# Attention values as the stationary operand of the probability products, two heads at a time, with transposed output, in a hybrid decoder layer; and a reordered entry of attention

## The chip, the cores and the metric

The kernel runs on one core of one Trainium2 chip. The metric is device time in microseconds. Five engines of the core have queues of their own and meet only at semaphores: TensorE (PE in the profile; PEld is its loading of the stationary operand), VectorE (DVE), ScalarE (ACT), GpSimd (POOL) and SyncE (SP), which here only issues transfers.

## The reference

One layer of a hybrid decoder on x (512 positions, 1024 features), all float32: RMS norm; one projection to all inputs of two mixers; (A) a gated linear recurrence, 4 heads of 128; (B) sparse attention, 8 heads of 64: an indexer scores all keys, each query keeps its best 128, and their logits get a bias by distance; the outputs of both mixers concatenated times W_o, normalised and added to x; then a SwiGLU feed-forward of 2816 hidden features, normalised and added. What the change is about:

```
p = softmax(logits)                    # per query, over the kept keys
y_B[q, h, :] = sum_k p[q, h, k] * v[k, h, :]
y = concat(y_A, y_B) @ w_o
```

## The kernel before

**Projections.** The 512 positions are 4 blocks of 128. Weights arrive in chunks of 1 MB (`chunks`, index j) through a ring of two raw buffers. Each is split in two float32r parts: ScalarE copies the rounded value to `w_hi`, VectorE subtracts to get `w_lo` (`split(j)`); a product with such operands takes three passes (`passes`). 33 `groups` of 128 features (24 passes of 512 columns each, some 5.5 us) are projected by `project(g)`; ScalarE and VectorE evacuate group g (`evac`, for keys and queries also `stack_lo`) out of PSUM bank g % 4. The last four groups, 29 to 32, are the attention keys, two heads each.

**Top-k.** VectorE finds the best 128 keys by 16 rounds for each of three query blocks (`topk_round`: maximum of eight, replace). `topk_share(g)` says how many of the 48 rounds VectorE does at each group from 7 on: three to group 12, then two. Groups 14 to 20 carry also the seven levels of the recurrence, for which VectorE (`advance`) and ScalarE (`level_operands`) prepare operands of TensorE (L1215).

**Attention** is a software pipeline over 32 units (b, h), `unit_order`, written out by hand in the same order on all engines. Step i (`attend(i)`) does, on TensorE: the logits of unit i (L1191, L1192); the probability product of unit i - 5 (L1333); the turning of unit i - 3's probabilities through the identity (L1344). GpSimd makes a tile of bias and mask for each unit (L523), three buffers. VectorE adds it and finds the row maximum (L993), ScalarE takes the exponential and its sum (L664), and the two alternate in copying turned probabilities to SBUF (L320, L667). In block b a unit has b + 1 tiles of 128 keys.

The product of a unit has the turned probabilities as stationary operand (128 keys x 128 queries) and the 64 value columns moving; the block's result is y with queries on partitions. When all eight heads of a block are done (`block_done`), VectorE multiplies by the reciprocal sums (`y_norm_b`, L978 a reciprocal of 8 elements a partition, L982), TensorE turns the result by four transposes (`turn_y_b`, L1304), ScalarE and VectorE make its two parts for the output projection (`y_hi_b`, `y_lo_b`). The recurrence's parts (`y_hi_a`, `y_lo_a`) and the split of the first W_o chunk in quarters (`split_quarter`, L550 and L795) are placed at fixed steps.

Steps 0 to 5 of TensorE lie between the passes of the last group; ScalarE and VectorE do steps 0 to 4, then that group's evacuation, then go on.

**Down projection.** Eleven chunks; the last chunk is done for row blocks 0 to 3 in turn, block 3 in two halves of 512 columns. Each block is then squared on ScalarE, its inverse root taken on GpSimd (L442), multiplied (L1125, or L1131 for halves), scaled and added (L1135) on VectorE, and stored.

Of the kernel before, what the change touches and what calls it, by code (L numbers as in the profile page):

```python
# [34 lines left out]
def hymba_layer(nc, x, w_in, lb_logits, hgrn_gnorm, rel_bias, w_o, norm_pre_mix, norm_post_mix,  # L35
# [54 lines left out]
    EARLY = HEADS_B - 2  # L90
    unit_order = [(b, h) for b in range(TB) for h in range(HEADS_B)]
    unit_order[EARLY:EARLY + 5] = [(1, 0), (1, 1), (1, 2), (0, EARLY), (0, EARLY + 1)]
    Y_A_AT = {12 + 2 * h: h for h in range(HEADS_A)}
    QUARTER_AT = {22: 0, 24: 1, 26: 2, 28: 3}
    TURN_BANK = (4, 6, 4, 2)

    with ExitStack() as ctx:
# [13 lines left out]
        N1, N2 = FT * 2 * S, 7936  # L111
# [29 lines left out]
        rs = sb("rs", [P, UNITS])  # L141
# [22 lines left out]
        PT = [a1(21504 + 512 * i, 512) for i in range(2)]  # L164
        yb = [a1(2048, 512), a1(2560, 512)]
# [16 lines left out]
        raw_ikw = A2[:, 7296:7296 + KT * IKW]  # L182
        Bh = A2[:, 0:4096].rearrange("p (h c) -> p h c", h=HEADS_B)
# [74 lines left out]
        s_yb = sem("attention_y_normed")  # L258
        s_ybt = sem("attention_yT_psum")
# [4 lines left out]
        s_woq = sem("quarter_of_first_wo_hi")  # L264
# [22 lines left out]
        def qk_bank(i):  # L287
            return 6 if i % 3 == 2 and i < unit_order.index((0, EARLY)) else QK_BANK[i % 3]

# [77 lines left out]
        def slot_free(eng, j):  # L367
            before = [i for i in range(j) if w_slot(i) == w_slot(j)]
            if before:
                used(eng, before[-1])  # L370
            elif w_slot(j) == 2:
                eng.wait_ge(s_pv, UNITS)
# [166 lines left out]
        def _(act):  # L539
# [5 lines left out]
            def split_quarter(q):  # L545
                if q == 0:
                    raw_landed(act, J_WO)
                    slot_free(act, J_WO)
                cols = slice(q * CH // 4, (q + 1) * CH // 4)
                act.activation(w_hi[:, w_slot(J_WO), cols], raw[:, ring_of(J_WO) % 2, cols],  # L550
                               ACT.Copy).then_inc(s_hi if q == 3 else s_woq, 1)

# [44 lines left out]
            def evac(g):  # L597
# [13 lines left out]
                elif kind == "ak":  # L611
                    for e in range(2):
# [93 lines left out]
            for i in range(EARLY - 1, UNITS + PV_LAG):  # L706
                attend(i)
            y_hi_b(TB - 1)
# [67 lines left out]
        def _(dve):  # L776
# [12 lines left out]
            def split_quarter(q):  # L789
                if q == 3:  # L790
                    dve.wait_ge(s_hi, J_WO + 1)
                else:
                    dve.wait_ge(s_woq, q + 1)
                cols = slice(q * CH // 4, (q + 1) * CH // 4)
                o = dve.tensor_tensor(w_lo[:, w_slot(J_WO), cols], raw[:, ring_of(J_WO) % 2, cols],  # L795
                                      w_hi[:, w_slot(J_WO), cols].bitcast(F32), ALU.subtract)
                if q == 3:
                    o.then_inc(s_lo, 1)

# [116 lines left out]
            def stack_lo(g):  # L916
# [5 lines left out]
                for e in range(1 if kind == "ikw" else 2):  # L922
# [10 lines left out]
                o.then_inc(s_ev[g % 4], 1)  # L933
# [35 lines left out]
            def y_lo_b(b):  # L969
                dve.wait_ge(s_yhi, b + 1)  # L970
                dve.tensor_tensor(hT_lo[:, 4:8, b * P:(b + 1) * P],
                                  PS[:, 6, :].rearrange("p (k t) -> p k t", t=P),
                                  hT_hi[:, 4:8, b * P:(b + 1) * P].bitcast(F32), ALU.subtract).then_inc(s_ylo, 1)

            def y_norm_b(b):
                u = slice(8 * b, 8 * b + 8)
                dve.wait_ge(s_ex, ended(b))
                link(dve.reciprocal(rs[:, u], sm[:, u]))  # L978
                dve.wait_ge(s_pv, ended(b))
                if b >= 2:  # L980
                    dve.wait_ge(s_ybt, b - 1)
                dve.tensor_tensor(yb[b % 2].rearrange("p (h d) -> p h d", d=DH),  # L982
                                  PS[:, 4 + b % 2, :].rearrange("p (h d) -> p h d", d=DH),
                                  rs[:, u].unsqueeze(2).to_broadcast([P, HEADS_B, DH]), ALU.mult).then_inc(s_yb, 1)

            def attend(i):
# [12 lines left out]
                if i - 1 in QUARTER_AT:  # L999
                    split_quarter(QUARTER_AT[i - 1])  # L1000
                b = block_done(i - 1)
                if b is not None:
                    y_norm_b(b)
# [485 lines left out]
```

## Time and profile before

| | us |
|---|---|
| median of 3 timed runs (703.04, 706.20, 706.27) | 706.2 |
| profiled execution, own time | 704.14 |
| its span, first to last instruction | 702.4 |
| TensorE busy / VectorE / ScalarE / GpSimd | 685.9 / 381.9 / 259.8 / 93.9 |
| mean granted TensorE clock | 0.997 |

Busy times of engines overlap each other. On TensorE a record's end is modelled and lies over the start of the next record, so the distance of two starts is what a pass takes. An fp32 product is recorded as two matmuls, a transpose as one. "Idle before" is the time in which an engine had nothing running ahead of the instruction.

### The profile page before, as it was taken

The numbers are of one execution on the slowest core, as the hardware profiler recorded it, in microseconds if no ns is written. First come the engines' busy times: TensorE is split into PE (matmuls) and PEld (weight loads), VectorE is DVE, ScalarE is ACT, GpSimd is POOL, SyncE is SP. The second block draws the span as 40 slices with busy tenths as digits, with TensorE's granted clock in tenths as the row PEclk, the third lists the DMA queues.
The fourth block names the chain that finished last, engine by engine and source line by source line (L and its number), as shares of the span: only waits on it lengthen the run. The fifth ranks groups of instructions, "written<-read, shape, count | busy, mean of one in ns | idle before, by whom it ended". The sixth has DMA issues, their size and how long they took to land.

```text
span 702.4 us, 8568 instructions
## 1 busy us (share of the span) xinstructions
PE 685.9 (98%) x3472; PEld 579.0 (82%) x3472; DVE 381.9 (54%) x553; ACT 259.8 (37%) x401; POOL 93.9 (13%) x130
## 2 busy tenths in 40 slices
PE   8999999999999979999999999999999999999996
PEld 5978888888988878888988888888888888888884
DVE  3865999999668689337643343343433432212216
ACT  5656434444257377235532223133232231211213
POOL 1810220000407478002100000000000000000001
PEclk9999999999999999999999999999999999999998
DMA  8443042342521100351350332323313223233103
GB/s 261 122 150 87 35 120 61 105 159 67 181 61 60 61 1 30 152 185 55 97 170 9 115 114 68 119 75 105 120 61 119 96 85 119 64 116 112 69 0 120
DMA packets 49352, 68.59 MB, mean 98 GB/s; under 512 B 5025, under 2 KB 39841, under 8 KB 49314
## 3 DMA queue, kind: packets, MB, share of 16 engines
q1 hardware_dynamic: 44320, 60.07, 26.6%
q0 software_dynamic: 3280, 7.35, 3.0%
q10 hardware_dynamic: 1714, 0.64, 0.4%
q8 instruction: 27, 0.44, 0.2%
q14 instruction: 11, 0.09, 0.0%
HBM read 65.40 MB, written 4.74 MB: 100 GB/s over the span
## 4 chain that ended last, share of the span: by engine, by line
PE 81%; DVE 12%; ACT 4%; issue 3%; DMA 0%; POOL 0%; DVEq 0%; ACTq 0%
PE PS L1143 70%; PE PS L1333 2%; DVE w_lo L787 2%; DVE A L858 2%; DVE top L857 1%; DVE A L1031 1%; PE PS L1252 1%; PE PS L1215 1%; PE PS L1186 1%; PE PS L1344 1%; PE PS L1239 1%; PE PS L1192 1%; ACT A L702 1%; PE PS L1191 1%; PE PS L1276 1%
## 5 line engine op out<-in xcount | busy, mean ns | idle before, releaser
L1143 PE MATMUL PS<-hT_lo,w_hi 128*128 128x512 f32 (+2 forms) x584 | 218.3, 374 | 0.9 <-DVE w_lo L819 0.5
L1143 PE MATMUL PS<-hT_hi,w_lo 128*128 128x512 f32 (+2 forms) x584 | 217.2, 372 | 0.0
L1143 PE MATMUL PS<-hT_hi,w_hi 128*128 128x512 f32 (+2 forms) x584 | 217.2, 372 | 0.0
L787 DVE TENSOR_TENSOR w_lo<-raw,w_hi 128x2048 fp32r<-128x2048 f32 x49 | 114.5, 2336 | 176.0 <-ACT w_hi L543 175.7
L543 ACT ACTIVATE w_hi<-raw 128x2048 fp32r<-128x2048 f32 x49 | 93.8, 1914 | 210.2 <-PE PS L1143 209.5
L1143 PEld LDWEIGHTS PS<-hT_lo,w_hi 128*128 128x128 f32 (+1 forms) x584 | 109.7, 188 | 20.1 <-DVE w_lo L819 0.8
L1143 PEld LDWEIGHTS PS<-hT_hi,w_hi 128*128 128x128 f32 (+1 forms) x584 | 109.6, 188 | 19.5
L1143 PEld LDWEIGHTS PS<-hT_hi,w_lo 128*128 128x128 f32 (+1 forms) x584 | 109.7, 188 | 18.5
L1143 PE MATMUL PS<-w_hi,ff 128*128 128x512 f32 x352 | 108.2, 389 | 0.0
L1143 PEld LDWEIGHTS PS<-w_hi,ff 128*128 128x128 f32 x352 | 66.1, 188 | 13.7
L1143 PE MATMUL PS<-w_lo,ff 128*128 128x512 f32 x176 | 68.5, 389 | 0.0
L442 POOL TENSOR_TENSOR rstd<-ms,mhalf 128x1 f32<-128x1 f32 x16 | 10.3, 642 | 423.7 <-ACT ms L722 406.9
L1143 PE MATMUL PS<-w_lo,hT_hi 128*128 128x512 f32 x112 | 44.6, 398 | 0.0
L1143 PE MATMUL PS<-w_hi,hT_hi 128*128 128x512 f32 x112 | 43.7, 390 | 0.0
L1143 PE MATMUL PS<-w_hi,hT_lo 128*128 128x512 f32 x112 | 43.6, 390 | 0.0
L1104 DVE TENSOR_TENSOR A<-PS,A 128x512 f32<-128x512 f32 x22 | 15.2, 692 | 47.2 <-issue 27.6
L1143 PEld LDWEIGHTS PS<-w_lo,ff 128*128 128x128 f32 x176 | 33.0, 188 | 6.9
L931 DVE SCALAR_TENSOR_TENSOR QK<-PS,QK 64x512 fp32r<-64x512 f32 x33 | 22.7, 689 | 11.6 <-ACT QK L609 6.7
L857 DVE MAX8 top<-A 128x8 f32<-128x256 f32 (+2 forms) x48 | 26.7, 557 | 0.6
L523 POOL TENSOR_TENSOR A<-A 128x256 f32<-128x256 f32 (+2 forms) x24 | 26.0, 1105 | 7.2 <-DVE nm L993 6.9
L858 DVE MATCH_REPLACE8 A<-top,A 128x256 f32<-128x256 f32 (+2 forms) x48 | 26.0, 543 | 0.0
L1333 PEld LDWEIGHTS PS<-A 128*128 128x128 f32 x160 | 21.3, 191 | 4.9 <-ACT A L667 4.1
(170 smaller groups left out, 762.3 us busy)
## 6 DMA issues: line engine op xcount, KB each, us to landing
raw<-in_w_in_dram SPq DMA_DIRECT2D x16, 1024.0 KB, 5.6
raw<-in_w_gate_dram SPq DMA_DIRECT2D x11, 1024.0 KB, 5.2
raw<-in_w_up_dram SPq DMA_DIRECT2D x11, 1024.0 KB, 5.3
raw<-in_w_down_dram SPq DMA_DIRECT2D x11, 1024.0 KB, 4.9
raw<-in_w_o_dram SPq DMA_DIRECT2D x4, 1024.0 KB, 4.9
A<-in_x_dram SPq DMA_DIRECT2D x4, 512.0 KB, 5.6
A<-in_x_dram POOLq DMA_DIRECT2D x4, 512.0 KB, 7.4
out_dram<-A SPq DMA_DIRECT2D x8, 256.0 KB, 2.0
```

The lines of the kernel that those rows point to most:

```text
L442: pool.tensor_tensor(rstd[:, col:col + 1], ms[:, col:col + 1], mhalf[:, 0:1], ALU.pow).then_inc(s_rs, 1)
L523: pool.tensor_tensor(BM[u % 3][:, 0:n], M, Bh[:, h, (TB - 1 - b) * P:S], ALU.subtract).then_inc(s_bm, 1)
L543: act.activation(w_split(j)[0], raw_view(j), ACT.Copy).then_inc(s_hi, 1)
L702: o = act.activation(junk[:, i % 8 * DK:(i % 8 + 1) * DK], ya[:, i * DK:(i + 1) * DK], ACT.Square, accum_out=ss[:, 16 + i:17 + i])
L787: dve.tensor_tensor(lo, raw_view(j), hi.bitcast(F32), ALU.subtract).then_inc(s_lo, 1)
L857: link(dve.max(top8[:, :], SC[b]))
L858: link(dve.match_replace(SC[b], top8[:, :], SC[b], TAKEN))
L931: o = dve.scalar_tensor_tensor(out=t, in0=p, scalar=scale, in1=hi, op0=ALU.mult, op1=ALU.subtract)
L1031: o = dve.scalar_tensor_tensor(out=SC[b], in0=rl[u % 3][:, 0:n], scalar=iw[:, b, h:h + 1], in1=SC[b], op0=ALU.mult, op1=ALU.add)
L1104: dve.tensor_tensor(fraw[f % 2], PS[:, 2 + f % 2, :], sig[f % 2], ALU.mult).then_inc(s_fr, 1)
L1143: o = pe.matmul(out, lhs[a], rhs[b], start=(first and n == 0), stop=(last and n == 2))
L1333: o = pe.matmul(PS[:, 4 + b % 2, h * DH:(h + 1) * DH], PT[u % 2][:, s * P:(s + 1) * P], av[:, s * W + h * DH:s * W + (h + 1) * DH], start= ...
```

## The change

The product of a pair of units (h, h + 1) of one block is now issued together, at every second step: the values of one head (128 keys x 64) are stationary, the turned probabilities (128 queries) move. Head h writes PSUM partitions 0 to 63, head h + 1 partitions 64 to 127 (two halves of the array), so that the block's result comes out transposed. The turned probabilities get four buffers instead of two.

The transposes of y go. The reciprocal sums must now lie along the columns: VectorE writes them widened to 64 copies a head (`widen_sums`, a reciprocal with 128 x 512 outputs), TensorE turns them by four fp32 products with the identity (`spread_sums`), ScalarE copies them to SBUF (`take_sums`), and VectorE multiplies (`y_norm_b`).

The order of units is (0, 0..5), (1, 0..5), (0, 6..7), (1, 6..7), then blocks 2 and 3. Steps 0 to 3 lie between the passes of group 31, steps 4 to 8 between those of group 32 (`BESIDE`), with the evacuation of each in two halves around a step. The first W_o chunk is split whole, after group 30, and the recurrence's parts are made from step 23. `topk_share` gives one round a group from 13 to 20, and three from 22 to 25.

In the down projection the last two chunks are done together for each row block; all 24 passes of each half of block 3 come last.

```diff
-    EARLY = HEADS_B - 2
-    unit_order = [(b, h) for b in range(TB) for h in range(HEADS_B)]
-    unit_order[EARLY:EARLY + 5] = [(1, 0), (1, 1), (1, 2), (0, EARLY), (0, EARLY + 1)]
-    Y_A_AT = {12 + 2 * h: h for h in range(HEADS_A)}
-    QUARTER_AT = {22: 0, 24: 1, 26: 2, 28: 3}
+    unit_order = [(b, h) for b in (0, 1) for h in range(HEADS_B - 2)]
+    unit_order += [(b, h) for b in (0, 1) for h in (HEADS_B - 2, HEADS_B - 1)] + [(b, h) for b in range(2, TB) for h in range(HEADS_B)]
+    LAST_KEYS = unit_order.index((0, HEADS_B - 2))
+    BESIDE = {len(groups) - 2: (4, range(4)), len(groups) - 1: (3, range(4, 9))}
+    Y_A_AT = {23 + 2 * h: h for h in range(HEADS_A)}
...
-        PT = [a1(21504 + 512 * i, 512) for i in range(2)]
-        yb = [a1(2048, 512), a1(2560, 512)]
+        PT = [a1(21504, 512), a1(22016, 512), a1(2560, 512), a1(3584, 512)]
+        y_sb = [a1(2048, 512), A2[:, 7936:8448]]
...
         def turned_to_sbuf(eng, u, copy):
             n = (unit_order[u][0] + 1) * P
             eng.wait_ge(s_ptp, u + 1)
-            if u >= 2:
-                eng.wait_ge(s_pv, u - 1)
-            copy(PT[u % 2][:, 0:n], PS[:, 2 + u % 2, 0:n]).then_inc(s_pts[u % 2], 1)
+            if u >= 4:
+                eng.wait_ge(s_pv, (u - 4) // 2 + 1)
+            copy(PT[u % 4][:, 0:n], PS[:, 2 + u % 2, 0:n]).then_inc(s_pts[u % 2], 1)
...
-            def evac(g):
+            def evac(g, heads=(0, 1)):
...
+            def take_sums(b):
+                act.wait_ge(s_rps, b + 1)
+                if b >= 2:
+                    act.wait_ge(s_ylo, b - 1)
+                act.activation(y_sb[b % 2], PS[:, 6, :], ACT.Copy).then_inc(s_rsb, 1)
+
             def y_hi_b(b):
-                act.wait_ge(s_ybt, b + 1)
+                act.wait_ge(s_yb, b + 1)
                 act.activation(hT_hi[:, 4:8, b * P:(b + 1) * P],
-                               PS[:, 6, :].rearrange("p (k t) -> p k t", t=P), ACT.Copy).then_inc(s_yhi, 1)
+                               y_sb[b % 2].rearrange("p (k t) -> p k t", t=P), ACT.Copy).then_inc(s_yhi, 1)
 
...
-                if i in QUARTER_AT:
-                    split_quarter(QUARTER_AT[i])
-                b = block_done(i - 3)
+                b = block_done(i - 2)
+                if b is not None:
+                    take_sums(b)
+                b = block_done(i - 4)
                 if b is not None:
                     y_hi_b(b)
...
-                if g + 1 == len(groups):
-                    for i in range(EARLY - 1):
+                if g in BESIDE:
+                    units = BESIDE[g][1]
+                    for i in units[:-1]:
                         attend(i)
-                evac(g)
-                if last_of_chunk(g) and j + 2 < J_WO and j + 2 != AHEAD:
+                    evac(g, (0,))
+                    attend(units[-1])
+                    evac(g, (1,))
+                else:
+                    evac(g)
+                if last_of_chunk(g) and j + 2 <= J_WO and j + 2 != AHEAD:
                     split(j + 2)
...
             def topk_share(g):
-                if g < G_L0 - 1:
+                if g < G_L0 - 1 or G_OFF <= g <= G_YNORM:
                     return (1, 2) if last_of_chunk(g) else (2, 1)
-                return (1, 1)
...
             def y_lo_b(b):
                 dve.wait_ge(s_yhi, b + 1)
-                dve.tensor_tensor(hT_lo[:, 4:8, b * P:(b + 1) * P],
-                                  PS[:, 6, :].rearrange("p (k t) -> p k t", t=P),
+                dve.tensor_tensor(hT_lo[:, 4:8, b * P:(b + 1) * P], y_sb[b % 2].rearrange("p (k t) -> p k t", t=P),
                                   hT_hi[:, 4:8, b * P:(b + 1) * P].bitcast(F32), ALU.subtract).then_inc(s_ylo, 1)
 
+            def widen_sums(b):
+                dve.wait_ge(s_ex, ended(b))
+                if b:
+                    dve.wait_ge(s_rps, b)
+                dve.reciprocal(r_wide.rearrange("p (h d) -> p h d", d=DH),
+                               sm[:, 8 * b:8 * b + 8].unsqueeze(2).to_broadcast([P, HEADS_B, DH])).then_inc(s_rw, 1)
+
             def y_norm_b(b):
-                u = slice(8 * b, 8 * b + 8)
-                dve.wait_ge(s_ex, ended(b))
-                link(dve.reciprocal(rs[:, u], sm[:, u]))
-                dve.wait_ge(s_pv, ended(b))
-                if b >= 2:
-                    dve.wait_ge(s_ybt, b - 1)
-                dve.tensor_tensor(yb[b % 2].rearrange("p (h d) -> p h d", d=DH),
-                                  PS[:, 4 + b % 2, :].rearrange("p (h d) -> p h d", d=DH),
-                                  rs[:, u].unsqueeze(2).to_broadcast([P, HEADS_B, DH]), ALU.mult).then_inc(s_yb, 1)
+                dve.wait_ge(s_rsb, b + 1)
+                dve.wait_ge(s_pv, ended(b) // 2)
+                dve.tensor_tensor(y_sb[b % 2], PS[:, 4 + b % 2, :], y_sb[b % 2], ALU.mult).then_inc(s_yb, 1)
...
                 feature_group(w_split(0), m, P, m, S // 2, S, s_proj)
-            def turn_y_b(b):
-                pe.wait_ge(s_yb, b + 1)
-                if b >= 1:
-                    pe.wait_ge(s_ylo, b)
+            def spread_sums(b):
+                pe.wait_ge(s_rw, b + 1)
+                if b:
+                    pe.wait_ge(s_rsb, b)
                 for k in range(4):
-                    o = pe.transpose(PS[:, 6, k * P:(k + 1) * P], yb[b % 2][:, k * P:(k + 1) * P], ident[:, :])
-                o.then_inc(s_ybt, 1)
+                    o = pe.matmul(PS[:, 6, k * P:(k + 1) * P], r_wide[:, k * P:(k + 1) * P], ident[:, :],
+                                  start=True, stop=True)
+                o.then_inc(s_rps, 1)
...
+                if i >= PV_LAG and (i - PV_LAG) % 2:
                     u = i - PV_LAG
-                    b, h = unit_order[u]
-                    pe.wait_ge(s_pts[u % 2], u // 2 + 1)
-                    if u == 0:
+                    b, h = unit_order[u - 1]
+                    for e in range(2):
+                        pe.wait_ge(s_pts[e], u // 2 + 1)
+                    if u == 1:
                         for g in range(first_group["av"], first_group["av"] + 4):
                             evacuated(pe, g)
                     if h == 0 and b >= 2:
                         pe.wait_ge(s_yb, b - 1)
                     for s in range(b + 1):
-                        o = pe.matmul(PS[:, 4 + b % 2, h * DH:(h + 1) * DH], PT[u % 2][:, s * P:(s + 1) * P],
-                                      av[:, s * W + h * DH:s * W + (h + 1) * DH], start=(s == 0), stop=(s == b))
+                        for e in range(2):
+                            o = pe.matmul(PS[e * DH:(e + 1) * DH, 4 + b % 2, h // 2 * P:(h // 2 + 1) * P],
+                                          av[:, s * W + (h + e) * DH:s * W + (h + e + 1) * DH],
+                                          PT[(u - 1 + e) % 4][:, s * P:(s + 1) * P], start=(s == 0), stop=(s == b))
                     o.then_inc(s_pv, 1)
...
                     elif c == 0 and t == 1:
                         pe.wait_ge(s_pts[0], UNITS // 2)
                         pe.wait_ge(s_pts[1], UNITS // 2)
+                        spread_sums(TB - 1)
                     elif c == 0 and t == 2:
-                        turn_y_b(TB - 1)
+                        pe.wait_ge(s_yb, TB)
                     elif c == 0 and t == 3:
                         pe.wait_ge(s_ylo, TB)
...
+            C_LAST = FT // 2 - 1
+            for c in range(C_LAST - 1):
                 pe.wait_ge(s_lo, J_DN + c + 1)
                 pe.wait_ge(s_flo, 2 * c + 2)
...
+            pe.wait_ge(s_flo, FT)
+            pe.wait_ge(s_lo, J_DN + C_LAST)
+            for t in range(2):
+                row_block(J_DN + C_LAST - 1, 2 * C_LAST - 2, ff_parts, t, False, False)
+            pe.wait_ge(s_lo, J_DN + C_LAST + 1)
+            for t in range(2):
+                row_block(J_DN + C_LAST, 2 * C_LAST, ff_parts, t, False, True).then_inc(s_dn, 1)
+            row_block(J_DN + C_LAST - 1, 2 * C_LAST - 2, ff_parts, 2, False, False)
+            row_block(J_DN + C_LAST, 2 * C_LAST, ff_parts, 2, False, True).then_inc(s_dn, 1)
+            t = TB - 1
+            for half in range(2):
+                for k in range(2 * C_LAST - 2, 2 * C_LAST + 2):
+                    w = w_split(J_DN + k // 2)
+                    o = passes(k, [x[:, t * P:(t + 1) * P] for x in ff_parts(k)],
+                               [x[:, k % 2, half * 512:(half + 1) * 512] for x in w],
+                               PS[:, 2 * t + half, :], False, k == 2 * C_LAST + 1)
+                o.then_inc(s_dn, 1)
```

## Rows read from the trace of the kernel before

**Rows 1.** The page: busy time and share; shares of the chain that ended last.
```profile
PE 685.9 (98%) x3472; PEld 579.0 (82%) x3472; DVE 381.9 (54%) x553; ACT 259.8 (37%) x401; POOL 93.9 (13%) x130
...
PE 81%; DVE 12%; ACT 4%; issue 3%; DMA 0%; POOL 0%; DVEq 0%; ACTq 0%
```

**Rows 2.** Windows: stretch, busy us of PE, PEld, DVE, ACT, POOL; granted clock; DMA share.
```profile
160.00:175.00 15.00, 15.00 (x85) 12.99 (x84) 14.72 (x33) 5.44 (x7) 0.00 (x0) 1.00 0.24 71
190.00:205.00 15.00, 15.00 (x81) 12.88 (x80) 7.74 (x12) 3.60 (x5) 0.00 (x0) 1.00 0.05 13
240.00:288.00 48.00, 43.34 (x338) 39.96 (x337) 35.72 (x103) 33.37 (x94) 30.48 (x33) 1.00 0.17 67
```

**Rows 3.** What TensorE waited for over the whole span: us, times, longest.
```profile
PE PS L1333 <- ACT A L667: 3.0, 3, 2.0
...
PE PS L1304 <- DVE A L982: 1.7, 2, 1.1
PE PS L1215 <- ACT A L645: 1.5, 2, 0.8
```

**Rows 4.** TensorE in order of time in attention: start, length, [idle before <-releaser].
```profile
246.53 0.28 PE L1192 MATMUL PS<-QK 128*128 128x256 f32 x1
248.81 0.43 PE L1333 MATMUL PS<-A 128*128 128x64 f32 x2 [2.00 <-ACT A L667]
...
258.76 0.66 PE L1304 MATMUL PS<-ident,A 128*128 128x128 f32 x4 [1.09 <-DVE A L982]
...
263.65 0.55 PE L1333 MATMUL PS<-A 128*128 128x64 f32 x3 [0.77 <-ACT A L667]
...
279.37 0.66 PE L1304 MATMUL PS<-ident,A 128*128 128x128 f32 x4 [0.59 <-DVE A L982]
279.78 0.47 PE L1191 MATMUL PS<-QK 128*128 128x512 f32 x1
```

**Rows 5.** TensorE in order of time, two units of block 3.
```profile
281.15 0.61 PE L1344 MATMUL PS<-ident,A 128*128 128x128 f32 x4
281.59 1.00 PE L1333 MATMUL PS<-A 128*128 128x64 f32 x8
282.43 0.60 PE L1344 MATMUL PS<-ident,A 128*128 128x128 f32 x4
```

**Rows 6.** Line 1252, fp32 products of 128 columns: count, lengths, first and last start.
```profile
L1252 PE MATMUL PS<-A x80: 270/275/275, 183.7 to 192.6; 128*128 128x128 f32 x80
```

**Rows 7.** TensorE in order of time around the eight-row transposes.
```profile
52.09 0.39 PE L1143 MATMUL PS<-hT_hi,w_hi 128*128 128x512 f32 x1
52.41 0.41 PE L1199 MATMUL PS<-ident,A 8*128 8x8 f32 x4
```

**Rows 8.** VectorE by line and shape: count, busy us, mean ns, idle before.
```profile
L993 DVE CUSTOM_DVE_ANT_0 A<-PS,A 128x384 f32<-128x384 f32 x8 | 4.3, 551 | 0.9 <-PE PS L1192 0.8
...
L795 DVE TENSOR_TENSOR w_lo<-raw,w_hi 128x512 fp32r<-128x512 f32 x4 | 3.9, 978 | 0.6 <-ACT w_hi L550 0.5
...
L982 DVE TENSOR_TENSOR A<-PS,rs 128x512 f32<-128x512 f32 x4 | 2.8, 692 | 1.2 <-issue 1.1
...
L978 DVE RECIPROCAL rs<-sm 128x8 f32<-128x8 f32 x4 | 0.8, 192 | 0.0
...
L842 DVE RECIPROCAL lbw<-lbw 128x4 f32<-128x4 f32 x1 | 0.2, 178 | 0.0
```

**Rows 9.** GpSimd by line and shape from 236 to 300 us.
```profile
L523 POOL TENSOR_TENSOR A<-A 128x512 f32<-128x512 f32 x8 | 11.0, 1404 | 1.7 <-DVE nm L993 1.6
```

**Rows 10.** The end of the kernel in order of time.
```profile
695.84 0.60 ACT L765 ACTIVATE raw<-PS 128x512 f32<-128x512 f32 x1 [0.44 <-PE PS L1143]
...
696.93 0.65 POOL L442 TENSOR_TENSOR rstd<-ms,mhalf 128x1 f32<-128x1 f32 x1 [1.84 <-ACT ms L771]
697.09 1.41 DVE L1131 TENSOR_TENSOR raw<-PS,A 128x512 f32<-128x512 f32 x2
698.54 1.42 DVE L1135 SCALAR_TENSOR_TENSOR A<-raw,rstd,A 128x512 f32<-128x512 f32 x2
```

More of the change, by code:

```diff
@@ L287, in qk_bank @@
         def qk_bank(i):
-            return 6 if i % 3 == 2 and i < unit_order.index((0, EARLY)) else QK_BANK[i % 3]
+            return 6 if i % 3 == 2 and i < LAST_KEYS else QK_BANK[i % 3]
         def ended(b):
@@ L611, in evac @@
                 elif kind == "ak":
-                    for e in range(2):
+                    for e in heads:
                         act.activation(KS[0:DH, 2 * h + e, :], ps[e * DH:(e + 1) * DH, :], ACT.Copy).then_inc(s_sth, 1)
@@ L704, in _ @@
                     o.then_inc(s_ss, 1)
-            for i in range(EARLY - 1, UNITS + PV_LAG):
+            for i in range(9, UNITS + PV_LAG):
                 attend(i)
+            take_sums(TB - 1)
             y_hi_b(TB - 1)
@@ L921, in stack_lo @@
                 scale = -DH ** -0.5 if kind == "aq" else 1.0
-                for e in range(1 if kind == "ikw" else 2):
+                for e in heads[:1] if kind == "ikw" else heads:
                     dve.wait_ge(s_sth, before + (2 if kind == "ikw" else e + 1))
@@ L1035, in _ @@
                     split(j + 2)
-                if g + 1 == len(groups):
+                if g in BESIDE:
                     topk_rounds(48)
-                    for i in range(EARLY - 1):
+                    units = BESIDE[g][1]
+                    for i in units[:-1]:
                         attend(i)
-                evac(g)
+                    stack_lo(g, (0,))
+                    attend(units[-1])
+                    stack_lo(g, (1,))
+                else:
+                    evac(g)
                 if g >= G_TOPK:
@@ L1059, in _ @@
                     topk_rounds(topk_share(g)[1])
-            for i in range(EARLY - 1, UNITS + PV_LAG):
+            for i in range(9, UNITS + PV_LAG):
                 attend(i)
+            widen_sums(TB - 1)
             y_norm_b(TB - 1)
@@ L1159, in beside @@
                     return lambda k: indexer_dot(g, k)
-                if g + 1 == len(groups):
-                    return lambda k: attend(k + EARLY - KT) if k >= KT - EARLY else None
+                if g in BESIDE:
+                    k0, units = BESIDE[g]
+                    return lambda k: attend(units[k - k0]) if 0 <= k - k0 < len(units) else None
                 return None
@@ L1362, in _ @@
                     turn_y()
-            for i in range(EARLY, UNITS + PV_LAG):
+            for i in range(9, UNITS + PV_LAG):
                 attend(i)
@@ L1430, in _, with ff_parts @@
                     feature_group(w_split(j), m, P, 2 * up + m, S // 2 if c == 0 else 0, S, s_gu)
[L1431 removed]
+            def ff_parts(k):
+                return ff[:, k, 0, :], ff[:, k, 1, :]
+            C_LAST = FT // 2 - 1
+            for c in range(C_LAST - 1):
                 pe.wait_ge(s_lo, J_DN + c + 1)
                 pe.wait_ge(s_flo, 2 * c + 2)
[L1434 removed]
                 for t in (2, 3, 0, 1) if c == 0 else range(TB):
@@ L1438, in _ @@
                         pe.wait_ge(s_fr, FT)
-                    def acts(k):
-                        return ff[:, k, 0, :], ff[:, k, 1, :]
-                    if last and t == TB - 1:
-                        w = w_split(J_DN + c)
-                        for half in range(2):
-                            for kk in range(2):
-                                o = passes(kk, [x[:, t * P:(t + 1) * P] for x in acts(2 * c + kk)],
-                                           [x[:, kk, half * 512:(half + 1) * 512] for x in w],
-                                           PS[:, 2 * t + half, :], False, kk == 1)
-                            o.then_inc(s_dn, 1)
-                        continue
-                    o = row_block(J_DN + c, 2 * c, acts, t, c == 0, last)
-                    if last:
-                        o.then_inc(s_dn, 1)
-                if not last:
-                    o.then_inc(s_rows, 1)
+                    o = row_block(J_DN + c, 2 * c, ff_parts, t, c == 0, False)
+                o.then_inc(s_rows, 1)
+            pe.wait_ge(s_flo, FT)
[15 more added lines that the diff above has]
+                o.then_inc(s_dn, 1)
     return nc
```

52 lines of the change are left out of this document (18 added, 34 removed).

## The prediction

> **What bounds the kernel now.** Read the page first: TensorE is busy for 98% of the span, and the chain that ended last runs through it for 81% [rows 1]. So only two things can shorten this kernel: less work in TensorE's own queue, or fewer places where that queue stands. "Busy" hides both, because the end of a matmul is modelled; from here on durations on TensorE are distances between starts. Next the stretches: in attention (240 to 288 us) TensorE is busy 43.3 of 48 us, VectorE 35.7, ScalarE 33.4, GpSimd 30.5, at the full granted clock [rows 2]; nobody is far behind, so a cut on TensorE soon meets somebody else. Then the waits of TensorE: 3.0 us on ScalarE's copies of turned probabilities (L667), 1.7 us on VectorE's normalisation (L982), 1.5 us on the operands of the recurrence's levels (L645) [rows 3]. The timeline places those of attention: 2.00 us at unit 7, 1.09 at block 0's turn, 0.77 in block 2, 0.59 at block 2's turn [rows 4]. Each is really 0.16 us longer (the record before it, 0.28 us long, fills a slot of 0.12), which with a last small one makes 5.4 us of standing. The first comes because ScalarE does the last group's evacuation between the softmax of units 4 and 5 while TensorE has nothing but attention left.
>
> **1. The probability products.** 80 fp32 products are 160 passes (a product is recorded as two matmuls). Today the probabilities are stationary with 128 columns and 64 columns stream: eight passes take 281.59 to 282.43 = 0.84 us, 0.105 each, 16.7 us in all [rows 5]. In the new form 64 columns are stationary and 128 stream. A pass with 128 fp32 columns costs (192.6 - 183.7)/79 = 0.112 us [rows 6]; so passes one after another cost 17.9 us, a small loss. The gain is there only if the two halves run at once. The order issued is head 0 pass a, pass b, head 1 pass a, pass b: within a head b follows a, but head 1's a may lie beside head 0's b. A pair of units of block b has 4(b+1) passes and then takes 2(b+1)+1 slots: 3, 5, 7, 9 for blocks 0 to 3, four pairs each, 96 slots x 0.112 = 10.8 us. No row shows two halves at once, so the bounds are 10.8 and 17.9; I take 10.8, since nothing else here can be what the form is limited by once passes address different columns.
>
> **2. Changing the shape of the array in use.** Each of 16 pairs has a change in and one out. The nearest row: from a 512-column pass at 52.09 to eight-row transposes at 52.41 is 0.32 us where the pass itself fills 0.23, so 0.09 for a change [rows 7]. 32 x 0.09 = 2.9 us (bounds 0 and, at 0.2 each, 6.4). Part 1 and 2 together: 13.7 against 16.7, -3.0 us.
> The Trainium skill speaks against this part: TensorEngine Tiling (Array Packing), Key Properties, says that changing the tiling mode drains the engine, while tiles of one mode work independently. By the trace the nearest such change costs 0.09 us, a modest drain; the page gives no figure, and no run so far shows a change of column tiles.
>
> **3. Spreading the reciprocal sums.** Sixteen transposes (four take 279.37 to 279.78 [rows 4], 1.65 us in all) go; 16 fp32 products, 32 passes x 0.112 = 3.6 us, come: +1.9 us. TensorE's own work changes by -1.1 us.
>
> **4. The widened reciprocal on VectorE.** Now a reciprocal of 8 elements takes 192 ns, one of 4 takes 178 [rows 8]. The new one has 512. At one element a cycle it would be 0.69 us, like the multiply of that size [rows 8]; if the whole 192 ns were per-element cost it would be 12 us. The two reciprocals differ by 3.5 ns an element: 0.18 + 508 x 0.0035 = 2.0 us, which I take. Four of them, W each.
> VectorE: DVE Perf Modes, in the Trainium skill (its walkthrough of the 8-slice pipeline), says that a reciprocal is an iterative divide with a repeat count of 8. At the 0.96 GHz that the skill's Trainium Kernel Development and Optimization (NeuronCore Architecture) gives for VectorE that would be, as an estimate, 8.3 ns an element and 4.3 us. The rows, at 3.5 ns an element, agree only in direction; rival (b) is the one that this rule speaks for, and with 4.3 its sum would be some 2.4 us higher.
>
> **5. The waits in attention afterwards.** Block 0's sums are widened at step 19 and TensorE wants them at step 20. From the logits of unit 19, VectorE needs 0.55 (one reduction [rows 8]) + W + 0.1. TensorE's pieces: turning is 0.11 a tile [rows 5], so 0.3 for three; logits are two passes of 384 columns at 0.23 for 512 [rows 7], so 0.4; a pair of block 1 is 5 x 0.112 + 0.18 = 0.7. It turns, forms logits, multiplies and turns, 1.7, and stands W - 1.0. At step 22 the first product of block 2 needs block 0's normalised result out of the same bank, and VectorE has on the way two reductions, a copy as wide, block 1's widening and the multiply (0.69, L982 [rows 8]), and it first waits 0.3 for the second logits: 2.7 + W, against TensorE's 0.9 of spreading, 0.4, 0.3 and 0.4: it stands W + 0.7. For block 2, with four tiles, TensorE's cover is 2.5 us against 0.8 + W: W - 1.7. Block 3's widening lies beside 2.7 us of output projection and a pair of products: nothing below W = 3. With W = 2.0: 1.0 + 2.7 + 0.3 = 4.0 us.
> Entry: nine units instead of six are beside the last two groups, and evacuation is cut in two around a unit, so the 2.16 us stand shrinks. Behind the whole split of the first output-weight chunk after group 30, unit 0's softmax comes some 0.3 us late, and the two evacuation halves hold units 9 to 12 by some 0.5: 0.8 us. The 0.77 us at 263.65 is ScalarE's two copies of earlier y parts; these move later and apart: 0. Altogether 4.8 instead of 5.4: -0.6 us. Four added copies on ScalarE replace four quarter splits, 512 wide like them. VectorE loses 4 x 0.98 of quarter splits (L795 [rows 8]) in attention and gains 4 W: 4.1 us more, paid in the waits just counted. GpSimd needs 1.40 us for a bias tile of block 3 [rows 9] beside a unit of TensorE of about 1.5: it hides, barely.
>
> **6. Top-k rounds moved.** Eight rounds leave the level stage, where VectorE is busy 14.7 of 15 us, and go to where it is busy 7.7 of 15 [rows 2]. The waits on L645 are for operands that VectorE releases: a round less in every group removes both, -1.5 us [rows 3]. Were they due to ScalarE, nothing.
>
> **7. The tail.** After the last matmul (its square starts at 695.84) the inverse root is ready at 696.93 + 0.65 = 697.58, but VectorE reaches the last scaling at 698.54, because it was busy with block 2's and then with two multiplies from 697.09 [rows 10]. With 24 matmuls instead of 12 behind block 2, block 2 and the first half are done by then: scaling starts near 697.65, -0.9 us. The next-to-last weights are needed 5.4 us earlier relative to the last ones, whose split ends with about 1 us to spare.
>
> **Sum.** -1.1 - 0.6 - 1.5 - 0.9 = -4.1 us against the profiled execution's 704.1: 700.0. That execution lies 2.1 below the median shown; the four times known average 704.9, and I place the changed kernel from there: 700.8 us.
>
> **Rivals.**
> (a) A cheap widening, W = 0.7: step 22 stands 1.4, the others nothing, so the stands are 2.2, -3.2 against today, and the sum is -6.7: 698.2 us. For it: the reciprocal of 4 elements is hardly dearer than other tiny instructions; against: the slope.
> (b) VectorE becomes the bound: W = 3.7, twice the slope. Stands of 2.7, 4.4, 2.0 and 0.7 with the entry 0.8 make 10.6, +5.2 against today, and the sum is +1.7: 706.6 us.
> (c) The halves do not overlap (slower): the products cost 17.9 + 2.9 = 20.8, +4.1, the spreading +1.9. A longer pair covers more of the waits (4.2, so -1.2), the rest stands: +2.4, 707.3 us with W = 2.0, and some +8 with 3.7. It decides once the overlap saves less than 4 of its 7.1 us. For it: every pass in this trace starts only when its predecessor's columns are through. Against: here all passes use all columns.
> (d) The products cost what I say but the level waits and the entry's merely move: 702 to 703 us.
>
> **How the numbers follow.** Forecast 0.33, (a) 0.18, (b) 0.21, (c) 0.23, (d) 0.05. From no change a measurement can tell about 0.5%, 3.5 us. The forecast lies just beyond that: some 0.20 of its 0.33 is faster; with (a) and 0.06 from (b) to (d), 0.44. Slower: half of (c), a third of (b), 0.18. Same 0.38. The likeliest case alone spans 698.5 to 703; for 8 in 10, 697 to 708.5, between a cheap reciprocal and serial halves.
>
> **What would show it.** Starts of products of two heads less than 0.06 us apart on average for right, 0.11 for (c). The reciprocal's own row for W. The waits of TensorE on VectorE near block 0 and 1 for step 5; no wait on L645; the last scaling under 2 us after the last matmul. It would be wrong if a change of shape costs 0.2 us, or if one of the longer stands lowers the granted clock, which is 1.00 now even with a stand of 2.2 us.

## The result, and the profile after

The changed kernel takes 720.9 us (median of four runs, 719.9 to 724.5) where the kernel before takes 705.7: ratio 1.0243, 95% interval 1.0208 to 1.0278. By the ratio it is 17 us slower; the two medians alone, few runs each, lie 15.1 us apart, and against the 704.2 us that the kernel before takes in the experiments the distance is 16.7. The prediction said 4 us faster, and its range ended at 708.5. The profiled execution took 724.5 us, the slowest of the four.

The page after: its busy times, which answer to [rows 1], and the 40 slices of TensorE and of its granted clock:
```profile
PE 695.1 (96%) x3488; PEld 580.4 (80%) x3488; DVE 393.1 (54%) x550; ACT 262.2 (36%) x402; POOL 92.0 (13%) x130
...
PE   8999999999999777799999999999999999999996
...
PEclk9999999999999997999999999999999999999999
```
TensorE falls behind in slices 14 to 17, 235 to 307 us: attention. The waits of TensorE in 220 to 330 us (engine, tile and line, what it waited for: us, times, longest), which answer to [rows 3]:
```profile
PE PS L1308 <- DVE A L974: 5.0, 2, 3.2
PE PS L1195 <- DVE A L908: 4.1, 1, 4.1
PE PS L1340 <- DVE A L980: 3.6, 1, 3.6
PE PS L1352 <- ACT A L666: 2.6, 2, 2.2
PE PS L1340 <- DVE A L321: 2.2, 3, 0.9
PE PS L1195 <- DVE QK L926: 1.3, 1, 1.3
```
ScalarE was the first to be waited for; now it is VectorE. L974 is the widened reciprocal, L908 the gating multiplications of the recurrence's output, L980 block 0's normalisation. The waits on the level operands (L645 before) are gone, as forecast. VectorE by line and shape, from 226 to 320 us, has the price of the first:
```profile
L974 DVE RECIPROCAL A<-sm 128x512 f32<-128x512 f32 x4 | 13.4, 3345 | 0.0
L793 DVE TENSOR_TENSOR w_lo<-raw,w_hi 128x2048 fp32r<-128x2048 f32 x3 | 7.1, 2381 | 1.2 <-ACT w_hi L544 1.1
```
That is 3.35 us, 6.5 ns an element, where 2.0 us was taken. The second is shown in VectorE's order of time, with what the moved top-k rounds (L852 to L855) do to L908:
```profile
235.29 0.68 DVE L853 MATCH_REPLACE8 A<-top,A 128x512 f32<-128x512 f32 x1
236.00 0.43 DVE L855 TENSOR_SCALAR A<-A 128x512 f32<-128x512 f32 x1
236.46 2.73 DVE L908 SCALAR_TENSOR_TENSOR A<-PS,gn,A 128x512 f32<-128x512 f32 x4
```
The same multiplications in the kernel before:
```profile
231.83 2.73 DVE L913 SCALAR_TENSOR_TENSOR A<-PS,gn,A 128x512 f32<-128x512 f32 x4
```
They start 4.6 us later now. The search ends at 236.4 us, and only then does VectorE reach what the first logit waits for. TensorE in order of time (start, length, idle before and releaser), to be laid beside [rows 4]:
```profile
239.24 0.33 PE L1195 MATMUL PS<-QK 128*128 128x128 f32 x1 [4.11 <-DVE A L908]
...
248.35 0.30 PE L1195 MATMUL PS<-QK 128*128 128x128 f32 x1 [1.30 <-DVE QK L926]
...
255.67 0.44 PE L1340 MATMUL PS<-A 128*64 128x128 f32 x4 [0.89 <-DVE A L321]
...
258.95 0.41 PE L1352 MATMUL PS<-ident,A 128*128 128x128 f32 x2 [2.24 <-ACT A L666]
...
271.15 2.08 PE L1308 MATMUL PS<-ident,A 128*128 128x128 f32 x8 [1.89 <-DVE A L974]
...
278.43 1.55 PE L1340 MATMUL PS<-A 128*64 128x128 f32 x12 [3.57 <-DVE A L980]
...
298.17 1.99 PE L1308 MATMUL PS<-ident,A 128*128 128x128 f32 x8 [3.16 <-DVE A L974]
```
These seven stands are 17.2 us as recorded; the four of [rows 4] were 4.5. The last, the widening of block 2 with 3.16 us, is longer than the reciprocal alone explains; VectorE's rows ahead of it show why:
```profile
293.65 1.20 DVE L963 TENSOR_TENSOR hT_lo<-A,hT_hi 128x512 fp32r<-128x512 f32 x1
294.77 3.34 DVE L974 RECIPROCAL A<-sm 128x512 f32<-128x512 f32 x1
```
L963 makes the low part of one head of the recurrence, which the change moved to steps from 23 on; 1.2 us of it lie between the last maximum of the block and the widening. The stretches (busy us of PE, PEld, DVE, ACT, POOL; granted clock; DMA) show a second thing that was not there before:
```profile
240.00:248.00 8.00, 7.05 (x27) 5.46 (x25) 5.05 (x12) 3.11 (x11) 2.03 (x4) 0.79 0.39 133
248.00:262.00 14.00, 10.52 (x75) 8.39 (x77) 7.04 (x30) 7.69 (x28) 6.63 (x10) 0.95 0.00 0
262.00:275.00 13.00, 10.88 (x67) 8.19 (x63) 9.01 (x20) 6.52 (x20) 7.60 (x9) 0.79 0.01 2
275.00:285.00 10.00, 6.57 (x38) 5.52 (x40) 5.79 (x9) 3.62 (x11) 3.31 (x3) 0.66 0.00 1
...
295.00:308.00 13.00, 8.53 (x76) 6.98 (x75) 8.81 (x12) 4.42 (x10) 1.81 (x4) 0.87 0.43 161
```
The clock, 1.00 in [rows 2], now falls to half (1.2 instead of 2.4 GHz) for a few us behind several stands. A share of 0.79 over 8 us is 3.4 us at half clock; the five stretches together make some 20 us. Two passes of the same form at either level:
```profile
241.11 0.63 PE L1146 MATMUL PS<-hT_hi,w_lo 128*128 128x512 f32 x1
241.54 0.63 PE L1146 MATMUL PS<-hT_hi,w_hi 128*128 128x512 f32 x1
...
244.84 0.39 PE L1146 MATMUL PS<-hT_lo,w_hi 128*128 128x512 f32 x1
245.07 0.40 PE L1146 MATMUL PS<-hT_hi,w_lo 128*128 128x512 f32 x1
```
Starts stand 0.43 us apart at first and 0.23 later.

And the part the change is named after, two units of block 3 as in [rows 5], now one pair:
```profile
292.69 0.47 PE L1195 MATMUL PS<-QK 128*128 128x512 f32 x1
293.00 0.40 PE L1196 MATMUL PS<-QK 128*128 128x512 f32 x1
293.33 1.09 PE L1340 MATMUL PS<-A 128*64 128x128 f32 x16
294.35 0.66 PE L1352 MATMUL PS<-ident,A 128*128 128x128 f32 x4
```
Sixteen passes, 293.33 to 294.35: 1.02 us, where the two units took 2 x 0.84. Taken one by one, their starts in the trace stand two and two, head 0 and head 1 within 0.01 us and each two 0.11 us behind the last. The halves do overlap.

### The profile page after: what moved, and what is told of

It is laid out like the page before. It is cut to its first block, busy times and chain, and to the rows that moved or that the text cites. A ratio compares the mean times of both kernels' runs of the same rounds, so it can differ in the third digit from the quotient of the medians.

```text
span 722.7 us, 8617 instructions
## 1 busy us (share of the span) xinstructions
PE 695.1 (96%) x3488; PEld 580.4 (80%) x3488; DVE 393.1 (54%) x550; ACT 262.2 (36%) x402; POOL 92.0 (13%) x130
## 4 chain that ended last, share of the span: by engine, by line
PE 85%; DVE 7%; ACT 3%; issue 3%; POOL 1%; ACTq 0%; DVEq 0%; POOLq 0%
PE PS L1146 74%; PE PS L1219 2%; PE PS L1190 1%; PE PS L1256 1%; PE PS L1340 1%; PE PS L1195 1%; PE PS L1196 1%; DVE w_lo L793 1%; PE PS L1352 1%; DVE QK L926 1%; PE PS L1308 1%; DVE A L974 1%; POOL A L524 1%; DVE A L853 1%; DVE top L852 1%
## 5 line engine op out<-in xcount | busy, mean ns | idle before, releaser
L793 DVE TENSOR_TENSOR w_lo<-raw,w_hi 128x2048 fp32r<-128x2048 f32 x50 | 117.0, 2340 | 185.9 <-ACT w_hi L544 185.6
L544 ACT ACTIVATE w_hi<-raw 128x2048 fp32r<-128x2048 f32 x50 | 95.7, 1914 | 215.6 <-PE PS L1146 214.9
L663 ACT ACTIVATE A<-A,nm 128x128 f32<-128x128 f32 (+3 forms) x32 | 17.9, 560 | 30.0 <-DVE nm L989 29.6
L1195 PE MATMUL PS<-QK 128*128 128x256 f32 (+3 forms) x56 | 22.0, 394 | 5.4 <-DVE A L908 4.1
L852 DVE MAX8 top<-A 128x8 f32<-128x256 f32 (+2 forms) x48 | 26.7, 557 | 0.7
```

The costliest lines, as they stand in the source:

```text
L544: act.activation(w_split(j)[0], raw_view(j), ACT.Copy).then_inc(s_hi, 1)
L663: act.activation(Pb[i % 4][:, 0:n], Pb[i % 4][:, 0:n], ACT.Exp, bias=nm[:, i:i + 1], scale=-1.0, accum_out=sm[:, b * HEADS_B + h:b * HEADS ...
L793: dve.tensor_tensor(lo, raw_view(j), hi.bitcast(F32), ALU.subtract).then_inc(s_lo, 1)
L852: link(dve.max(top8[:, :], SC[b]))
L1195: pe.matmul(out, QS[:, h, b * P:(b + 1) * P], KS[:, kh, 0:(b + 1) * P], start=True, stop=False)
```

## The experiments

All were timed beside the kernel before (704.2 us there, so a ratio of 0.001 is 0.7 us; the changed kernel stands at 1.0243). Differences between two versions are taken from their ratios; with intervals of about 0.002 to 0.0035 on either side they are good to some 2 to 3.5 us.

**1. The reciprocal alone.** A reciprocal of 8 values, then a copy that widens it; all else as changed.
```diff
-dve.reciprocal(r_wide..., sm[:, 8*b:8*b+8].unsqueeze(2).to_broadcast([P, HEADS_B, DH]))
+link(dve.reciprocal(rs[:, u], sm[:, u]))
+dve.tensor_copy(r_wide..., rs[:, u].unsqueeze(2).to_broadcast([P, HEADS_B, DH]))
```


> Changed kernel, but the reciprocal is taken of 8 sums a partition and a plain copy widens it to 512. Theory 1 (the wide reciprocal of 3.35 us makes three stands of TensorE, 2.2, 3.6 and 3.2 us, and each also lowers the granted clock for some microseconds): the widening falls to 0.9 us, the three stands shrink by about 2.4 us each, the clock stays up behind them, together 9 to 12 us: 709 to 712 us. Theory 2 (the column halves and their changes of shape are what costs): the pairs of products are untouched, at most 3 us go: about 718 us.

Measured: 711.7 us, ratio 1.010 (1.0064 to 1.0135): 10 us back (give or take 3.5). TensorE's waits on the widening and the normalisation shrink, the one on the gating stays:
```profile
PE PS L1198 <- DVE A L909: 4.1, 1, 4.1
...
PE PS L1343 <- DVE A L983: 1.2, 1, 1.2
...
PE PS L1311 <- DVE A L977: 0.5, 1, 0.5
```
Dividing 512 times instead of 8 in each partition is the largest single cause, by the middle value more than half.

**2. The moved top-k rounds alone, put back.**
```diff
-if g < G_L0 - 1 or G_OFF <= g <= G_YNORM:
+if g < G_L0 - 1:
     return (1, 2) if last_of_chunk(g) else (2, 1)
-return (1, 0) if g < G_ENDS else (1, 1)
+return (1, 1)
```


> Changed kernel with the top-k rounds shared out over the groups as in the kernel before. Theory 1 (the moved rounds stand in front of the gating of the recurrence's output, for which step 0 of attention now waits 4.1 us and then runs at half clock): that stand and the half clock behind it go, 5 to 6 us, the two waits of the levels come back, 1.5 us: 716 to 717 us. Theory 2 (the stand comes from starting attention a group earlier whatever the order of VectorE): the stand stays above 3 us: 720 us or more.

Measured: 717.6 us, ratio 1.0184 (1.0148 to 1.022): 4 us back. The wait of 4.1 us is gone, and a wait of 1.3 us for level operands is back.

**3. Both.**

> Both edits together. Theory 1, if the two causes are independent: the sum of both savings, 703 to 707 us. Theory 2: 714 us or more.

Measured: 706.8 us, ratio 1.0032 (1.0018 to 1.0047). The two make 15 of the 17 us; what is left is still slower than before, though TensorE has less work.

**4. The entry of attention as before, on top of 3.** Six units beside the last group instead of nine beside two, each evacuation whole, and an order of units like the one before that keeps pairs together.
```diff
-BESIDE = {len(groups) - 2: (4, range(4)), len(groups) - 1: (3, range(4, 9))}
+BESIDE = {len(groups) - 1: (2, range(6))}
```


> Both edits, and the entry of attention as before: six steps beside the last group alone, its evacuation whole after step 4 (unit order adapted so that pairs stay together). Theory 1 (the earlier entry gains no time, because evacuations now hold the softmax of the units beside them): the waits of steps 4, 8 and 9 go and the single one of 2.2 us at step 7 comes back: 0 to 3 us less than the run without this edit. Theory 2 (the earlier entry is worth the 2 us that it was to save): 1 to 3 us more than that run.

Measured: 701.4 us, ratio 0.9951 (0.9931 to 0.9971). The new entry costs 5.7 us, more than the 0 to 3 of the first theory. The forecast had it the other way round: 0.8 us in place of a stand of 2.16, a gain of 1.4.

**5. Half of the entry: the early start kept, each evacuation whole (against 3).**
```diff
-for i in units[:-1]: attend(i)
-evac(g, (0,)); attend(units[-1]); evac(g, (1,))
+for i in units: attend(i)
+evac(g)
```


> Narrow reciprocal and old top-k shares with the new early entry (steps 0 to 8 beside groups 31 and 32), but the evacuation of each of the two groups whole, behind all its steps. Theory 1 (cutting the evacuation around a step makes ScalarE and VectorE wait for each other in turn, four hand-overs for one step, which gives the waits of 1.0 and 2.3 us at steps 8 and 9): 2 to 3 us less than 706.8: 704 us. Theory 2 (starting a group earlier is itself the loss): 706 us or more.

Measured: 703.9 us, ratio 0.9997 (0.9981 to 1.0013). So cutting the evacuation in two costs 2.5 us, and the early start 3.2 more. No single line shows either, but the sum of TensorE's waits in attention does for the most part: 7.9 us in 3, 6.0 here, 3.7 in 4. That with the cut ScalarE's and VectorE's halves of an evacuation and a unit's softmax wait for one another in turn is a reading; no run shows it apart.

**6. The order within a pair, on top of 4:** head outside, key tile inside, so that head 1's passes are issued behind all of head 0's.
```diff
-for s in range(b + 1):
-    for e in range(2):
+for e in range(2):
+    for s in range(b + 1):
```


> The last kernel (narrow reciprocal, old top-k shares, old entry) with one edit: a pair's products are issued head by head, all passes of the first head and then all of the second, instead of head by head within each key tile. Theory 1 (two passes on different halves of the columns run at once only where they are neighbours in the queue): a pair of block 3 takes about 16 x 0.112 = 1.8 us instead of 1.02, 6 to 7 us more in all, of which waits hide a part: 705 to 708 us. Theory 2 (TensorE finds the overlap whatever the order, or the saving came from the shorter stationary operand): no change, 701 us.

Measured: 703.4 us, ratio 0.9986 (0.9969 to 1.0004), 2.5 us more than 4: less than expected. A pair of block 3 in this kernel:
```profile
275.26 1.58 PE L1339 MATMUL PS<-A 128*64 128x128 f32 x16
276.77 0.66 PE L1351 MATMUL PS<-ident,A 128*128 128x128 f32 x4
```
It takes 1.51 us, between 1.02 (all overlapped) and 1.8 (none). One by one in the trace, head 0's eight passes start 0.11 us apart from 275.26, and head 1's first starts at 275.75, beside head 0's fifth: some passes of the second half start beside the first half's even when issued behind them. Rival (c) is dead either way, and the issued order is worth 0.5 us a pair of four tiles.

**7. The top-k rounds spread otherwise, on top of 4.** One a group in groups 13 to 20, where the level operands are made, and four in 21 to 24, before the gating.
```diff
 if g < G_L0 - 1:
     return (1, 2) if last_of_chunk(g) else (2, 1)
-return (1, 1)
+if g < G_ENDS:
+    return (1, 0)
+return (2, 2) if g < G_ENDS + 4 else (1, 1)
```


> The kernel with the old entry, top-k shares so that one round a group stands beside the levels, four a group from 21 to 24, two from 25, so that the last round comes no later than before. Theory 1 (the moved rounds were harmful only where they stood in front of the gating): the two waits of the levels (1.5 us) go and nothing comes: 699.5 to 700.5 us. Theory 2 (the time is given back, since VectorE is full until group 29 anyway): 701 to 702 us.

Measured: 699.0 us, ratio 0.9914 (0.9887 to 0.9941). This version beats both kernels. What is left of TensorE's waits in attention:
```profile
PE PS L1353 <- ACT A L667: 2.3, 3, 2.0
PE PS L1341 <- DVE A L322: 0.9, 1, 0.9
...
PE PS L1309 <- DVE A L977: 0.5, 1, 0.5
```

**8. The same rounds and the tail in the kernel before, without the halves.**

> The kernel before with the new order of the last two down chunks and the same top-k shares as the previous kernel, nothing else. Theory 1: tail 0.9 and levels 1.5 us less than before: 702 us where the kernel before takes 704.2; the rest of the distance to the previous kernel, about 2 us, is what the column halves and the later recurrence parts bring. Theory 2 (the column halves bring nothing net of the spreading): it takes the same as the previous kernel.

Measured: 701.9 us, ratio 0.996 (0.9942 to 0.9977). Of the 6 us that 7 gains, 3 are the rounds' and the tail's. The other 3 (give or take 2) belong to all that still differs: the halves with a cheap reciprocal, four buffers for turned probabilities, the order of units, the whole split of the first W_o chunk and the later recurrence parts. No run takes the halves alone.

**9. The moved rounds alone in the kernel before.**

> The kernel before with one part of the change alone, the moved rounds of the top-k (three a group in groups 25 to 28, fewer in 13 to 20). Theory of the prediction (its step 6): -1.5 us, the waits of the levels, nothing given back: 704. Theory of the runs so far: the levels' 1.5 us go, and the rounds run until about 236 us in front of the gating multiplications on VectorE, which then end near 239 instead of 234.6; the first logits of this kernel come two steps into the last projection group, later than in the changed one, so less of the 4.5 us of delay lands on TensorE, 0.5 to 2 us: 704.5 to 706.5.

Measured: 702.9 us, ratio 0.9987 (0.9968 to 1.0006), less than either theory had. The interval touches no change, and the ten times fall in two groups of five, 701.3 to 701.9 and 703.8 to 706.3, so the gain of some 1 us is not shown. (The groups with three rounds are 22 to 25, and not 25 to 28 as the expectation has it.) The gating multiplications start at 234.85 instead of 231.83, and TensorE waits for nothing of it:
```profile
PE PS L1333 <- ACT A L667: 3.0, 3, 2.0
...
PE PS L1304 <- DVE A L982: 1.7, 2, 1.1
...
PE PS L1191 <- DVE nm L993: 0.3, 1, 0.3
```
Over the whole span the last line of [rows 3] is gone, and in attention only 0.3 us on a unit's maximum is new. It is close: the multiplications end at 237.58 and the first logit starts at 237.63. The moved rounds do no harm that can be measured by themselves; they do it together with an entry that wants the gated values six steps of a projection group earlier (step 4 of the last group but one instead of step 2 of the last).

**10. The tail alone in the kernel before.**

> The kernel before with the new order of the last down-projection chunks alone. Theory (the prediction's step 7): the last token tile's four rows stand together, so the other tiles' closing work is done earlier and the end of the kernel comes 0.9 us after less: 704.7 to 705.0 where the kernel before has 705.7, ratio 0.9985. Rival: the order makes TensorE wait for the chunks' splits once, which eats it: no change.

Measured: 703.2 us, ratio 0.9988 (0.9973 to 1.0002). The middle is the forecast's, but the interval touches no change. The changed kernel's trace shows it directly, beside [rows 10]:
```profile
717.08 0.60 ACT L771 ACTIVATE raw<-PS 128x512 f32<-128x512 f32 x1 [1.80 <-PE PS L1146]
...
718.17 0.54 POOL L443 TENSOR_TENSOR rstd<-ms,mhalf 128x1 f32<-128x1 f32 x1 [4.57 <-ACT ms L777]
718.82 1.41 DVE L1138 SCALAR_TENSOR_TENSOR A<-raw,rstd,A 128x512 f32<-128x512 f32 x2 [0.26 <-POOL rstd L443]
```
From the last square to the last scaling are 1.74 us instead of 2.70.

**11. The clock.** The changed kernel with transposes of the identity in TensorE's stands.
```diff
+keep_busy((len(groups) - 5) % 4, 36)      # 36 transposes of the identity
 pe.wait_ge(s_yg, TB)                      # the gated values
...
+keep_busy(6, (18, 18, 30, 0)[b])
 pe.wait_ge(s_rw, b + 1)                   # the widened reciprocal
...
+keep_busy(6, (30, 10)[b - 2])
 pe.wait_ge(s_yb, b - 1)                   # the normalised output
```
Two waits for a free bank are taken a little earlier for it; the rest is as changed.

> The changed kernel with work for TensorE in its stands and nothing else changed: 36 identity transposes (0.11 us each) ahead of the first logit's wait for the gated values, 18, 18 and 30 ahead of the waits for the widened reciprocal, 30 and 10 ahead of the waits for the normalised output. The transposes' results are never read. The waits themselves and everything on VectorE stay. In the changed kernel TensorE stood 4.5, 2.2, 3.9 and 3.4 us at these places and then ran at half its clock for stretches: granted clock 0.79 in 240 to 248 us, 0.79 and 0.66 in 262 to 285, 0.87 in 295 to 308. Theory A: the lowered clock costs time of its own, since TensorE's passes that follow are on the path: 512-column passes at 427 instead of 227 ns for 3.3 us are 1.5 us, and the stretches of attention 2 to 4 us more; with the clock held at 1.00 the kernel comes to 715 to 718 us. Theory B: VectorE's and ScalarE's chain sets the pace of the attention, and a slow TensorE there costs nothing: 720 to 722 us with the granted clock at 1.00. If the clock still falls, the filling was too short and the run tells nothing on either.

Measured: 721.4 us, ratio 1.0245 (1.0218 to 1.0272), the changed kernel's own. Its stretches:
```profile
240.00:248.00 8.00, 5.44 (x27) 4.07 (x26) 4.04 (x15) 3.60 (x13) 2.76 (x5) 1.00 0.34 131
248.00:262.00 14.00, 10.87 (x69) 8.37 (x68) 6.13 (x26) 7.90 (x27) 6.80 (x10) 0.78 0.01 1
262.00:275.00 13.00, 12.89 (x106) 11.08 (x106) 11.20 (x20) 6.41 (x19) 7.57 (x8) 0.97 0.01 3
275.00:285.00 10.00, 9.49 (x90) 7.83 (x89) 6.07 (x15) 4.54 (x11) 3.82 (x3) 1.00 0.00 0
```
The granted clock is back at 0.97 to 1.00 where it was 0.66 and 0.79, though it now falls in 248 to 262, where stands were left unfilled. By the condition put down beforehand (if the clock still falls, the run tells nothing) this is not a clean test; but the time at half clock in attention went from some 20 us to some 7, and the kernel's time does not move, where theory A had 3 to 6 us less. What the slow clock cost in the passes was mostly slack, time that TensorE would have waited out: behind the first stand it reached unit 3 earlier and stood there instead, a new wait:
```profile
PE PS L1195 <- DVE nm L989: 1.2, 1, 1.2
```
One profile against one would say otherwise (720.8 against 724.5 us), but 2.0 us of that lie ahead of attention (first logit at 237.28 against 239.24), where the two kernels are the same, and the medians agree. Up to some 3 us of clock, what the two intervals leave, can't be excluded.

## Why the prediction was wrong, step by step

**Steps 1 and 2, the products: right.** A pair of block 3 was to take 9 slots and two changes, 1.01 + 0.18 = 1.19 us. It takes 1.02 with the change out in it, and the change in adds 0.10 (293.00 to 293.33, less the pass's 0.23). The heads' passes run beside each other from the first, not shifted by one: 1.02 us is eight slots of 0.11, 0.05 more behind the first passes, and the change out. The Trainium skill (TensorEngine Tiling (Array Packing), Key Properties) says that a change of tiling mode drains the engine and that tiles of one mode work independently. The trace agrees: the change is about 0.1 us each way here, and the two halves start together.

**Step 3, spreading: right at full clock only.** With the cheap reciprocal the eight passes of a block take 0.8 to 0.9 us (experiment 1, starts 268.01 to 268.82 and 285.89 to 286.81), by 0.9 forecast. In the changed kernel the clock was at half for three of the four blocks, and they took 1.6 to 1.7.

**Step 4, W: mis-sized.** The term was 2.0 us, and it measures 3.35. The slope of 3.5 ns an element came from reciprocals of 4 and 8 elements, where the fixed part hides it. The real one is 6.5 ns. The price on which rival (b) stood, 3.7, was the nearer; so was the estimate from VectorE: DVE Perf Modes in the Trainium skill (repeat count of 8, 4.3 us), though it is too high by a quarter. Put into the formulas, 3.35 gives stands of 2.35, 4.05, 1.65 and 0.35 us. The trace has, from the last start before each stand to the next and less that pass's own slot, 2.05, 3.74 and 3.32 for the first three. The first two come out within 0.3 us. Block 2's is 1.7 too long: the formula left out the recurrence's low part, 1.2 us on VectorE (L963) directly ahead of that widening. With W right, the sum would have been about 705 (700.8 + 4.4): no reciprocal of this price explains 721 by itself. Between 3.35 and the 0.64 us of the cheap form (0.20 for the division, 0.44 for the copy) the formulas give 8.4 - 1.3 = 7.1 us, and experiment 1 measured 10; of the rest some 1 us is block 2's stand, which is longer than the formula has it, and what is left lies within the interval.

**Step 6, top-k: half right, and the step that failed.** The level waits went, 1.5 us by the rows, though experiment 9's gain of some 1 us is not clear of its interval. "Go to where it is busy 7.7 of 15" was read from a window of 190 to 205 us; the moved rounds reach until 236, past the gating multiplications that the first logit needs. The step failed by what it left out: who is behind the rounds in VectorE's queue. It forecast a gain of 1.5 us; with the early entry the rounds cost 4 to 5 (experiments 2 and 3).

**Step 5, the waits: failed.** The entry term of 0.8 us, which was to replace a stand of 2.16, counted what evacuation and softmax do to one another for units 9 to 12, and left out what the early start has to wait for: step 0 needs the gated values. With 6 there, 4.1 us of waiting; without it, still 5.7 us of cost (experiments 4 and 5): 2.5 from the cut, 3.2 from the start. That more units beside the groups do not help because VectorE and ScalarE set the pace there is my reading; no run takes their work away.

**Step 7, the tail: right,** 0.96 by the trace for 0.9.

**The clock** was named as what could make the forecast wrong. It fell, and cost nothing that can be measured.

Together: reciprocal 10, rounds with the early start 5, entry otherwise 6 us, and against them 3 to 4 of gain, make the 17.

Laid beside the forecast, the miss of 21 us (4 faster forecast, 17 slower measured) has three terms. The reciprocal was priced at 2.7 us over the cheap form (stands of 4.0 instead of 1.3) and cost 10: 7 us. The rounds were to gain 1.5 and, in front of the gating, cost 4 to 5: 6 us. The entry was to gain 1.4 and cost 5.7: 7 us. What remains of the forecast, the products, the spreading and the tail with the cheap reciprocal, the old entry and the old rounds, would be 3.9 us of gain by its own numbers, and experiment 4 measured 3.4.

## What to carry to other kernels

A broadcast operand saves memory, and the reciprocal's work stays: divide the 8 values first and widen by a copy (0.20 + 0.44 us instead of 3.35). Before work is moved later in an engine's queue, or a consumer earlier, list what stands behind it in that queue up to the next thing that the busiest engine needs: the moved rounds, harmless with the old entry, and the earlier start met here in one wait of 4.1 us. And once stands are long, an engine's slower clock may be an effect and not the cause; fill the stands, all of them, and see whether the time moves.

## What the runs showed of the hardware

- VectorE's reciprocal: 195 ns for 128x8 (experiment 1), 3345 ns for 128x512 (changed kernel), so (3345 - 195)/504 = 6.25 ns an element at the margin.
- fp32 products in two column halves run side by side: 16 passes of 128 columns in 1.02 us (changed kernel); issued one head behind the other they still overlap in part (1.51 us, experiment 6).
- TensorE's granted clock fell to half for some 3.4 us behind a stand of 4.1 us, and for stretches behind others of 1.9 to 3.6 us as recorded; a stand of 2.0 us as recorded in the kernel before left it at 1.00.
